# Dealing the rows of an expert pass to every eighth SBUF partition instead of to consecutive ones

## What is computed

```python
topv, topi = lax.top_k(h @ w_router + b_router, 4)
gates = softmax(topv)
# for each expert e, for the tokens that chose it:
gu = xb @ w1[e] + b1[e]                       # w1: 1024 x 2048 in float32, 8 MB
gate, up = min(gu[:, :1024], 7), clip(gu[:, 1024:], -7, 7)
act = (up + 1) * (gate * sigmoid(1.702 * gate))
y[token] += gate_of_token * (act @ w2[e] + b2[e])   # w2: 1024 x 1024, 4 MB
```

## Time and profile before

| | |
|---|---|
| time, median of 3 runs | 1448.91 us (1445.15 to 1449.09) |
| time of the profiled execution | 1449.26 us |
| its span | 1447.7 us |
| PE busy | 1243.1 us, 86% |
| DVE, ACT, POOL busy | 46%, 34%, 15% |
| mean rate of all DMA | 331 GB/s over the span |

### The profile page before, as it was taken

One profiled execution on the slowest core, in us unless ns is written; L12 is line 12 of the kernel. 1 busy time (PEld: TensorE's weight loads), 2 busy tenths in 40 slices (PEclk: granted clock), 3 DMA queues, 4 the chain that ended last, 5 costly groups with the idle time before them and its releaser, 6 DMA issues.

```text
span 1447.7 us, 17440 instructions
## 1 busy us (share of the span) xinstructions
PE 1243.1 (86%) x6432; PEld 737.6 (51%) x6432; DVE 662.1 (46%) x958; ACT 488.2 (34%) x703; POOL 219.1 (15%) x301
## 2 busy tenths in 40 slices
PE   5798778974889998899899979999779999997970
PEld 2353445543267563666475427556447555742640
DVE  2530662345379554343486224426434444841631
ACT  5110430222057443233464223324333343731420
POOL 2211321012111021110311102012101021110101
PEclk9699888985899999899999989999989999999975
DMA  8930676214999999998999999999999999999975
GB/s 284 381 112 5 215 273 236 96 64 156 370 414 410 402 401 399 391 396 340 378 411 406 403 392 397 364 363 408 399 393 404 358 354 410 407 409 406 410 283 136
DMA packets 112793, 479.10 MB, mean 331 GB/s; under 512 B 12315, under 2 KB 13510, under 8 KB 82956
## 3 DMA queue, kind: packets, MB, share of 16 engines
q1 hardware_dynamic: 99020, 447.26, 78.0%
q0 software_dynamic: 13344, 29.60, 8.0%
q10 hardware_dynamic: 344, 1.12, 0.2%
HBM read 461.20 MB, written 24.01 MB: 335 GB/s over the span
## 4 chain that ended last, share of the span: by engine, by line
PE 49%; DMA 11%; SPq 8%; DVE 3%; issue 1%; ACT 1%; POOL 0%; POOLq 0%; DVEq 0%; ACTq 0%
PE bank L2233 47%; DMA raw<-in_w 8%; SPq L512 5%; SPq L522 2%; DMA yd<-ost,slot_tok 2%; DVE rawr L2084 1%; PE bank L2282 1%; PE bank L2259 1%; SPq L518 1%; DMA yd<-gu,slot_tok 1%; ACT hi L1905 1%; DMA yf<-yd 0%; DVE gu L2048 0%; DVE gu L2046 0%; DMA xg_even<-h2d,slot_tok 0%
## 5 line engine op out<-in xcount | busy, mean ns | idle before, releaser
L2084 DVE TENSOR_TENSOR rawr<-raw,hi 128x1024 fp32r<-128x1024 f32 x288 | 341.6, 1221 | 152.9 <-ACT hi L1905 149.9
L1905 ACT CAST hi<-raw 128x1024 fp32r<-128x1024 f32 x288 | 294.9, 1049 | 184.3 <-PE bank L2233 117.8
L2233 PE MATMUL bank<-raw,xT_even 128*64 128x512 f32 (+1 forms) x640 | 129.5, 608 | 0.0
L2233 PE MATMUL bank<-raw,xT_odd 128*32 128x512 f32 (+1 forms) x640 | 103.4, 703 | 26.4 <-DMA raw<-in_w 26.4
L2233 PE MATMUL bank<-raw,aT 128*32 128x256 f32 (+1 forms) x1024 | 108.0, 453 | 12.5 <-DMA raw<-in_w 12.4
L1801 POOL DMA_INDIRECT yd<-ost,slot_tok x32 | 56.5, 1765 | 371.5 <-ACT ost L1890 371.2
L2233 PE MATMUL bank<-hi,xTh_even 128*128 128x512 f32 x288 | 97.3, 420 | 8.1 <-DVE rawr L2084 8.1
L2233 PE MATMUL bank<-rawr,xTh_even 128*128 128x512 f32 x288 | 93.4, 407 | 0.0
L2233 PE MATMUL bank<-hi,xTl_even 128*128 128x512 f32 x288 | 93.0, 405 | 0.0
L2233 PE MATMUL bank<-hi,aTh 128*128 128x512 f32 x240 | 78.0, 407 | 9.4 <-DVE rawr L2084 9.3
L2233 PEld LDWEIGHTS bank<-raw,aT 128*32 128x32 f32 (+1 forms) x1024 | 41.2, 120 | 70.0 <-issue 32.3
(11 more groups left out here) (344 smaller groups left out, 1691.6 us busy)
## 6 DMA issues: line engine op xcount, KB each, us to landing
raw<-in_w SPq DMA_DIRECT2D x360, 1024.0 KB, 17.9
raw<-in_w_ada SPq DMA_DIRECT2D x24, 1024.0 KB, 6.4
raw<-in_w SPq DMA_DIRECT2D x48, 512.0 KB, 12.1
w_in_sb<-in_w_in SPq DMA_DIRECT2D x1, 5120.0 KB, 17.5
w_out_sb<-in_w_out SPq DMA_DIRECT2D x4, 1024.0 KB, 6.1
xs<-in_x_prompt SPq DMA_DIRECT2D x4, 512.0 KB, 17.0
yd<-zero POOLq DMA_DIRECT2D x4, 512.0 KB, 10.5
yf<-yd SPq DMA_DIRECT2D x4, 512.0 KB, 5.2
```

Of the source, the lines that this page charges most:

```text
L1905: nc.scalar.copy(m.hi[:, (2 * n + h) % HI, :], m.raw[:, slot, h * D:(h + 1) * D]).then_inc(hi_done, 1)
L2084: v.tensor_tensor(m.rawr[slot][:, half], m.raw[:, slot, half], m.hi[:, (2 * n + h) % HI, :].bitcast(F32), ALU.subtract).then_inc(lo_done, 1)
L2233: return nc.tensor.matmul(out, lhsT, rhs, start=start, stop=stop, skip_group_check=True)
```

## The change

The row of constants `1, 2, 3, ...` is replaced by a permuted one, for each capacity its own. No operation is added, taken away or moved: every engine issues the same instructions on the same shapes in the same order. The only shape that differs is the constants' own load before the experts begin (`rows_sb<-in_rows`, 128 x 352 values before and 128 x 448 now), and the tiles behind `rows_sb` in SBUF lie 384 bytes further.

```diff
-C_KEY, C_RANK, C_NO, C_SLOT = 0, NE, 2 * NE, 3 * NE
-N_ROWS = 3 * NE + 256
+C_KEY, C_RANK, C_NO = 0, NE, 2 * NE
+C_SLOT = {"A": 3 * NE, "B": 3 * NE, "C": 3 * NE + 256, "D": 3 * NE + 320}
+N_ROWS = 3 * NE + 352
...
-                at, slot = m.pcol[:, p % 4, :] if p else m.posm[:, 0, :], row(C_SLOT, n)
+                at, slot = m.pcol[:, p % 4, :] if p else m.posm[:, 0, :], row(C_SLOT[c], n)
...
-    rows[0, C_SLOT:C_SLOT + 256] = 1 + np.arange(256)
+    for c, n in (("B", P), ("C", 64), ("D", 32)):
+        spread = 1 + np.arange(n).reshape(n // 8, 8).T.reshape(-1).argsort()
+        rows[0, C_SLOT[c]:C_SLOT[c] + n] = spread
+    rows[0, C_SLOT["A"] + P:C_SLOT["A"] + 2 * P] = P + rows[0, C_SLOT["A"]:C_SLOT["A"] + P]
```

More of the change, by code:

```diff
@@ L2208, in one @@
                 v.scalar_tensor_tensor(m.oh[:, :, 0:P], m.pcol[:, 0, :].unsqueeze(2).to_broadcast([P, TT, P]), m.bcol[:, 0:1],
-                                       row(C_SLOT, P).unsqueeze(1).to_broadcast([P, TT, P]), ALU.subtract,
+                                       row(C_SLOT["B"], P).unsqueeze(1).to_broadcast([P, TT, P]), ALU.subtract,
                                        ALU.is_equal).then_inc(oh_ready, 1)
```

## The result

| | before | after |
|---|---|---|
| median of 8 runs each | 1447.12 us (1443.07 to 1449.89) | 1456.29 us (1447.93 to 1459.34) |
| ratio, 95% interval | | 1.0058 (1.0039 to 1.0077) |
| profiled execution, its span | 1449.26 us, 1447.7 us | 1458.38 us, 1456.8 us |

The change is slower by 0.4 to 0.8%, and the forecast (1448.9, range 1443 to 1454) was wrong: the time lies above the range, on a side that had a chance of 8%. Three later sets of 12 runs of the same kernel gave 1.0030 (1.0010 to 1.0049), 1.0041 (1.0022 to 1.0060) and 1.0032 (1.0013 to 1.0050). The mean of the four is 1.0040, or 5.8 us. That is the size to explain; the first set was the largest of the four. How far the time missed the range is partly chance: two of the three later medians, 1452.91 and 1451.03 us, lie inside 1443 to 1454, and the third, 1454.32 us, just above. The side is not: all four intervals lie above 1.

What follows compares the result with a forecast made beforehand. Weight loads on the 16 DMA engines set the pace, the most loaded engine counting; 1449.26 - 0.4 - 0.4 + 0.3 + 0.5 = 1449.3, less 0.35 us from profile to median: 1448.9 us, range 1443 to 1454.

Steps and rivals of the forecast that it cites:

- The longer load of the constants ... 0: Constants' load before the experts: issued at 232.1 us, takes 5.7, first read at 350.3, so covered: 0.
- the sum that follows: Whole kernel: 1449.26 - 0.4 - 0.4 + 0.3 + 0.5 = 1449.3, less 0.35 us for the runs' median: 1448.9 us.
- Ties ... I take +0.5: DMA-bound stretches: eight level engines, so other packets hitting any of them count; bounds 0 to +4.9 us, taken +0.5.
- The rival in the prediction: Last DMA-bound stretch: eight level engines, C passes included, make it slower, past +0.3% (1453.7 us); chance 7%.
- The map of engines: Row transfers: engine 8 x (p >> 6) + ((p >> 2) & 7) serves partition p, so every eighth partition lies on every second engine.
- The plateau: End of the weights: DMA share goes to about 0.5 (eight engines, 200 GB/s) for about 10 us, then 0.
- The rival of evened load: Row work beside weights: the deal evens the engines' load, gaining 17 to 22 us (1427 to 1432); chance 7%.
- the prices of the prediction: Row work, scatter plus gather: 0.49 us per 4 KB row, 0.25 per 2 KB part, 0.14 per 1 KB part.
- Pass 31's scatter: Last scatter, uncovered at the kernel's end: lands in 4.9 instead of 5.32 us, -0.4 us.
- Pass 0's wait: PE's wait for the first gather: most loaded engine goes from 4 to 8 parts, +0.3 us, +0.7 at twice the price.
- PE's wait for weights: Experts' part, 365 to 1410 us: stays at 38.8 us within 3.
- Pass 30's scatter: Scatter of 70 rows: eight rows on the most loaded engine either way, so it takes as long as before.

Runs made afterwards that it cites:

- e1: The changed kernel, unedited, timed again beside the kernel before: 1452.91 us, 1.0030.
- e2: The changed kernel with its longer table and layout, but filled with places 1, 2, 3, ... so no row moves: 1451.93 us, 1.0026 against before.
- e3: The changed kernel with rows dealt over all 16 engines by the engine map instead, longer table kept: 1435.63 us, 0.9914 against before.
- e4: The changed kernel with the C passes' rows in consecutive partitions again, B and D dealt as in the change: 1448.66 us, 1.0003 against before.
- e6: The kernel before with 96 unused values behind the constants in SBUF, so tiles lie 384 bytes further: 1448.43 us, 1.0003.
- e9: The changed kernel again, unedited, in a third session on another chip: 1454.32 us, 1.0041 against before.
- e10: Repeat of e2 (longer table filled with 1, 2, 3, ...) in the third session: 1448.83 us, 1.0016 against before.
- e12: Repeat of e4 (the change with plain C passes) in the third session: 1449.24 us, 1.0006 against before.
- e16: The changed kernel, its table and shift kept, with only the C passes dealt; B, A, D consecutive: 1447.85 us, 1.0026 against before.
- e17: The changed kernel again, unedited, run in turn with e18 on one chip: 1451.03 us, 1.0032 against before.
- e5: The kernel before, unaltered, run against itself as a null: 1447.60 us, 0.9999.
- e7: The kernel before with only the constants' row in HBM longer by 96 values that are not loaded: 1447.56 us, 1.0000.
- e8: The change's deal without its longer table: the compare reads the kernel before's constants in permuted order, no tile moved: 1448.10 us, 1.0007 against before.
- e11: Deal over all 16 engines as in e3, by reading the plain constants in permuted order, no tile moved: 1433.90 us, 0.9908 against before.
- e13: The changed kernel with its C and D tables in a tile behind everything else, so no tile moves: 1448.20 us, 1.0012 against before.
- e14: The changed kernel with 32 more unused values, so tiles lie 512 instead of 384 bytes further: 1449.89 us, 1.0016 against before.
- e15: Deal over all 16 engines as in e3, with C and D tables in e13's separate tile, so no shift: 1431.41 us, 0.9896 against before.
- e18: e14's kernel again (tiles 512 bytes further), run in turn with e17 on one chip: 1449.45 us, 1.0016 against before.

## Why the prediction was wrong

**The step that failed: "The longer load of the constants ... 0", and the sum that follows.** The load is indeed hidden. What the same edit also did, to move every tile behind `rows_sb` by 384 bytes, was written down in the section on the change and has no term in the sum. Before, the tile with the stationary operand `xTh` begins at byte 175104 of each partition, a multiple of 512 (342 x 512); after, at 175488, which is none. `xTl`, `aTh` and `aTl` move with it; the moving operands `hi` and `rawr` lie ahead of `rows_sb` and stay. The matmuls of the split A and B passes come at 233.3 ns instead of 229.2 in every one of the programs with that shift (after, e1, e2, e3, e4, e6, e9, e10, e12, e16, e17) and in none of the others (before, e5, e7, e8, e11, e13, e14, e15, e18). There are 3 x (288 + 192 + 240) = 2160 of them, and some 1,930 follow the one before at that pace: 1,930 x 4.1 ns = 7.9 us. Some of it is taken back by shorter waits between units; PE is busy with these matmuls for 537.0 us on average in the shifted programs and 531.2 in the others, 5.8 us more. Where PE never waits, as in passes 25 to 28, that time is lost (240 such matmuls x 4.1 ns = 1.0 us, and 0.9 measured); where the weights set the pace, PE's delay is hidden or regained, and without the deal the end stretch is even shorter with the shift (247.5 to 247.7 against 248.6 to 248.8 us). What reaches the end of the kernel is 0.27% or 3.9 us together with the deal (1.0040 against 1.0013); without it the sets have 0.15% or 2.2 us, which is not clear of nothing. That the shift slows the matmuls, and that it makes a good part of the change's loss, is shown: three ways of undoing it, e8, e13 and e14, bring back the 229 ns and most of the time, and e14 does so with a shift that is larger. It is the start modulo 512 bytes that was varied, with two values, and with all four stationary tiles, `gu` and `oh` moving at once; at which other offsets PE is slow wasn't tried. The mechanism inside PE isn't known.

**A term that may be too small: "Ties ... I take +0.5".** With aligned tiles the deal costs 1.0013 on the mean of four sets, 1.9 us, with an interval of about 0.1% either way, and the sum had nothing in all for it (-0.4 - 0.4 + 0.3 + 0.5). That is at the edge of what can be told, and of the right sign for eight level engines: 1.9 us lies inside the bounds of 0 to 4.9 that the term had. The traces put 0.5 us of it into the end stretch, and 2.1 us where the tiles are shifted. The rival in the prediction named that place and the C passes, and both are borne out: taking C's deal from the change takes its whole loss (1.0040 to 1.0003 and 1.0006) and 2.5 us of the end stretch. But C's deal is not enough by itself: alone it has 1.0026, against 1.0015 for the shift with no deal, and 0.2 us in the end stretch. By the map the C passes' parts then lie on the same eight engines as the dealt rows of the B passes. That the mechanism is ties with packets of other work is argued only, since no run took these packets away.

**What stays open.** Shift and deal alone add up to 2.2 + 1.9 = 4.1 us; the change has 5.8. That the two are worse together is measured in the end stretch: there the deal costs 1.6 us more with the shift than without. A plain mechanism would be that a PE that is later for the weights has less slack for a late engine, but no run tests it. Nor is it clear why the shift without C's deal comes to 1.0003, 1.0003 and 1.0006 (e6, e4, e12) and with the plain table to 1.0026 and 1.0016 (e2, e10): all five have the same pace of the matmuls, and their spread is about what single sets have. How the rest of the 5.8 us, ahead of pass 23, divides between shift and deal can't be told, since there the traces of one kernel differ by some 3.5 us.

**What held.**

- The map of engines, and so the first half of the argument: the deal puts the rows on every second engine and leaves the most loaded engine with as much as before. The plateau of 0.52 and 209 GB/s was to be 0.5 and 200 for 10 us; it is there for about 8. The Trainium skill (DMA: Bandwidth & Descriptors, section The descriptor swizzle) gives the same map, and the plateau, pass 0's gather, the last scatters and e3 agree with it.
- The rival of evened load was rightly put aside for this change, and its price was somewhat too high. It was 17 to 22 us for an even deal; the deals that are in fact even gave 12.4 (e3), 13.3 (e11) and 15.1 us (e15). The first carries the shift. The most loaded engine's row work goes from 86 to 68 us by the prices of the prediction, 18 us; in e15 3.3 us of the gain are the last two scatters alone (11.34 - 8.06), the rest comes with the weights.
- Pass 31's scatter: 4.93 us, forecast 4.9 (4.86 to 5.01 in the other traces with the change's deal of D, but 3.70 in e8, which nothing here explains). Pass 0's wait: +0.5 us, forecast +0.3 to +0.7. PE's wait for weights: 36.7 us, forecast 38.8 within 3. Pass 30's scatter: 6.26 against 6.02 us, forecast no change. The two scatters of an A pass: 10.7 to 12.3 and 10.3 to 12.0 us in the chains of 20 traces, with no order by deal (before has 11.48 and 11.34, after 11.60 and 11.95, e17 11.31 and 10.82).

The range was at fault too. It took in the bounds of each named term, and nothing for an effect that the diff showed and the argument did not price. The views that I had named as the test of the forecast would all have passed it: each was a wait, a share or a scatter, and a good part of the loss was in the busy time of PE.

## What to carry to other kernels

A constant that grows by some bytes moves every tile behind it: look where the operands of the matmuls begin before and after, and keep stationary tiles of 128 columns, 512 bytes a partition, at such multiples (here 229.2 against 233.3 ns each; the narrower ones of the C passes moved too, and their matmuls kept their pace), with a tail tile or some padding. Read the share of the DMA engines at the end of a long load: steps or a plateau mean that the side traffic is uneven. Their size is not what an even deal can give: in before the idle share of the two last windows is (0.34 + 0.63) x 4 = 3.9 us, and the even deals gave 12 to 15. To even rows over the engines deal them by the map, engine 8 x (p >> 6) + ((p >> 2) & 7), over all 16, not by a stride; that is a table of constants, and was worth 1.0% here.

## What was not expected of the hardware

- The start of the stationary tiles in SBUF shows in the rate of the matmuls that use them: 233.3 to 233.4 ns from start to start with `xTh` at 175488, 229.2 to 229.4 with it at 175104 or 175616, in 11 and 9 traces, 128x512 each, with nothing waiting.
- A gather is bound to engines by partition just as a scatter: pass 0's, which runs alone, keeps PE waiting 5.03 to 5.13 us with eight parts on its most loaded engine and 4.56 to 4.67 with four. With both dealt evenly beside the weights the kernel is 12 to 15 us faster.
- The start of the experts' part differs by up to 9 us from profile to profile (the first unit of weights is used up at 358.8 to 368.0 us over 20 traces), more than the effect of this change, and with no clear order by shift or deal.
